# Transposing the gated product of nine FFN steps in 32x32 blocks on VectorE, with the blocks exchanged through memory

## What is computed

```
D_MODEL = 1024; SEQ = 256; DEPTH = 2; D_FF = 2816

def swiglu(x, w_in, w_out):
    gu = x @ w_in
    g, u = jnp.split(gu, 2, axis=-1)
    return (jax.nn.silu(g) * u) @ w_out
...
    for l in range(DEPTH):
        x = x + 0.5 * swiglu(rms_norm(x, ffn1_norm[l]), ffn1_w_in[l], ffn1_w_out[l])
        x = x + mixer(...)
        x = x + 0.5 * swiglu(rms_norm(x, ffn2_norm[l]), ffn2_w_in[l], ffn2_w_out[l])
...
        gate, up = jnp.split(h2 @ w_gate_up[l], 2, axis=-1)
        x = x + (jax.nn.silu(gate) * up) @ w_down[l]
```

## Time and profile before

| what | value |
|---|---|
| time, median of 3 runs | 1720.64 us (1720.05 to 1723.21) |
| span of the profiled execution | 1721.5 us |
| PE busy | 1671.8 us, 97% of the span |
| DVE busy | 943.5 us, 55% |
| ACT busy | 803.8 us, 47% |
| POOL busy | 97.1 us, 6% |
| DMA | 308.96 MB, 179 GB/s on average |

### The profile page before, as it was taken

How to read it: one execution, slowest core, us unless ns; L and a number is a source line. 1 busy time by engine, 2 the same in 40 slices (tenths; PEclk the granted TensorE clock), 3 DMA queues, 4 the chain that set the end, 5 groups by cost and what they waited for, 6 DMA issues and landing times.

```text
span 1721.5 us, 22066 instructions
## 1 busy us (share of the span) xinstructions
PE 1671.8 (97%) x7760; PEld 1376.7 (80%) x7760; DVE 943.5 (55%) x843; ACT 803.8 (47%) x899; POOL 97.1 (6%) x105
## 2 busy tenths in 40 slices
PE   6999999999999999999999999899999999999998
PEld 5887887888888787888888888787888878788886
DVE  4545545575545645465566545566554556665454
ACT  5443454544434543444455444465444446544443
POOL 2010000010000002000001000021100002110000
PEclk9999999999999999999999999999999999899999
DMA  8875453446565578555345655644456564336552
GB/s 259 295 221 175 172 190 123 139 156 199 176 208 188 175 251 240 174 173 181 111 152 166 203 188 194 240 127 129 141 190 200 179 195 144 125 127 201 189 192 89
DMA packets 209187, 308.96 MB, mean 179 GB/s; under 512 B 10400, under 2 KB 153504, under 8 KB 208480
## 3 DMA queue, kind: packets, MB, share of 16 engines
q1 hardware_dynamic: 208272, 305.18, 54.1%
q0 software_dynamic: 560, 1.84, 0.4%
q10 hardware_dynamic: 288, 1.05, 0.2%
HBM read 306.97 MB, written 2.88 MB: 180 GB/s over the span
## 4 chain that ended last, share of the span: by engine, by line
PE 90%; DVE 3%; ACT 3%; issue 2%; DMA 1%; POOL 1%; DVEq 0%; SPq 0%; ACTq 0%; POOLq 0%
PE pg L1380 19%; PE pg L1381 18%; PE pg L1382 18%; PE acc L1382 9%; PE acc L1380 9%; PE acc L1381 9%; PE pg L1451 2%; DVE wlo L970 2%; ACT whi L671 1%; DMA raw<-in_ffn_w_in 1%; PE pg L1393 1%; PE acc L1530 1%; PE acc L1550 1%; POOL ms L590 0%; PE acc L1538 0%
## 5 line engine op out<-in xcount | busy, mean ns | idle before, releaser
L970 DVE TENSOR_TENSOR wlo<-raw,whi 128x2048 fp32r<-128x2048 f32 x277 | 641.2, 2316 | 513.8 <-ACT whi L671 513.8
L671 ACT ACTIVATE whi<-raw 128x2048 fp32r<-128x2048 f32 x277 | 529.5, 1913 | 338.6 <-PE pg L1382 168.2
L1380 PE MATMUL pg<-whi,xTh 128*128 128x512 f32 (+1 forms) x1456 | 580.3, 399 | 9.9 <-DVE wlo L970 5.7
L1382 PE MATMUL pg<-whi,xTl 128*128 128x512 f32 (+1 forms) x1456 | 570.4, 392 | 0.0
L1381 PE MATMUL pg<-wlo,xTh 128*128 128x512 f32 (+1 forms) x1456 | 570.2, 392 | 0.0
L1380 PEld LDWEIGHTS pg<-whi,xTh 128*128 128x128 f32 x1456 | 276.3, 190 | 73.6 <-DVE wlo L970 9.8
L1382 PEld LDWEIGHTS pg<-whi,xTl 128*128 128x128 f32 x1456 | 276.0, 190 | 57.5
L1381 PEld LDWEIGHTS pg<-wlo,xTh 128*128 128x128 f32 x1456 | 276.5, 190 | 54.3
L1380 PE MATMUL acc<-whi,bTh 128*128 128x512 f32 (+1 forms) x572 | 229.6, 401 | 0.0
L1382 PE MATMUL acc<-whi,bTl 128*128 128x512 f32 (+1 forms) x572 | 224.3, 392 | 0.0
L1381 PE MATMUL acc<-wlo,bTh 128*128 128x512 f32 (+1 forms) x572 | 223.1, 390 | 0.0
(11 more groups left out here) (159 smaller groups left out, 1048.2 us busy)
## 6 DMA issues: line engine op xcount, KB each, us to landing
raw<-in_ffn_w_in SPq DMA_DIRECT2D x176, 512.0 KB, 4.8
raw<-in_ffn_w_out SPq DMA_DIRECT2D x88, 512.0 KB, 4.0
raw<-in_w_gate_up SPq DMA_DIRECT2D x88, 512.0 KB, 4.7
raw<-in_mix_w_in SPq DMA_DIRECT2D x64, 512.0 KB, 4.1
raw<-in_w_down SPq DMA_DIRECT2D x44, 512.0 KB, 4.0
raw<-in_w_in SPq DMA_DIRECT2D x24, 512.0 KB, 4.8
raw<-in_mix_w_o SPq DMA_DIRECT2D x16, 512.0 KB, 4.7
raw<-in_w_o SPq DMA_DIRECT2D x16, 512.0 KB, 4.5
```

Of the source, the lines that this page charges most:

```text
L671: act_e.activation(whi[:, slot, :], raw[:, slot, :], ACT.Copy).then_inc(s.w_hi_ready, 1)
L970: v.tensor_tensor(wlo[:, slot, :], raw[:, slot, :], f32(whi[:, slot, :]), ALU.subtract).then_inc(s.w_lo_ready, 1)
L1380: pe.matmul(dst, xh, wh, start=first and i == 0, stop=False)
L1382: mm = pe.matmul(dst, xl, wh, start=False, stop=last and i == len(pairs) - 1)
```

## The change

In each FFN the transposes by PE stay for steps 0 and 10 only. For steps 1 to 9 (`TURNED` = 9) the transpose is done in three moves. DVE transposes `act` within blocks of 32x32 into `turned` (`v.transpose`, one instruction over 128x512 elements), after the product of tile 1 and ahead of the low part of slot 0. ACT's queue then stores `turned` (256 KB) to a buffer in memory, `act_blocks`, waits for the store, and issues four loads of 32 partitions x 4 pieces x 512 bytes (64 KB each) that bring the blocks to their places in `moved` (`move`, after the refill of slot 0). After the refill of slot 1, ACT waits for the four loads and writes the high part from `moved` (`moved_hi`), DVE the low part (`moved_lo`); both used to stand ahead of the refill of slot 1. The high and low parts lie in another order in `bTh` and `bTl` (tile and channel block exchanged), under the names `actTh` and `actTl`.

```diff
+        turned, moved = area(11264, TT * FB), area(11776, TT * FB)
+        act_blocks = act.rearrange("p t (c b j) -> p b (t c) j", c=2, b=QUADS)
+        turned_blocks = turned.rearrange("p (b n i) -> p b n i", b=QUADS, n=TT * 2)
+        moved_blocks = moved.rearrange("p (a e) -> p a e", a=QUADS)
+        moved_T = moved.rearrange("p (a n i) -> p n a i", a=QUADS, n=TT * 2)
...
+        stored = nc.dram_tensor("act_blocks", (QUADS, Q, QUADS, TT * FB // QUADS), F32, kind="Internal").ap()
...
+                def moved_hi(j, par):
+                    act_e.wait_ge(s.act_moved, 16 * QUADS * (TURNED * f + j))
+                    act_e.activation(actTh[:, par].rearrange("p n (a i) -> p n a i", a=QUADS), moved_T,
                                      ACT.Copy).then_inc(s.actT_hi, 1)
...
+                def move(j):
+
+                    act_e.wait_ge(s.act_turned, TURNED * f + j)
+                    act_e.dma_start(stored.rearrange("a j b e -> (a j) (b e)"), turned).then_inc(s.act_stored, 16)
+                    act_e.wait_ge(s.act_stored, 16 * (TURNED * f + j))
+                    act_e.wait_ge(s.actT_lo, STEPS * f + j)
+                    for b in range(QUADS):
+                        act_e.dma_start(moved_blocks[Q * b:Q * (b + 1)], stored[:, :, b, :].rearrange("a j e -> j a e"))\
+                            .then_inc(s.act_moved, 16)
...
+                def moved_lo(j, par):
+                    v.wait_ge(s.actT_hi, STEPS * f + j + 1)
+                    hi, lo = (b[:, par].rearrange("p n (a i) -> p n a i", a=QUADS) for b in (actTh, actTl))
+                    v.tensor_tensor(lo, moved_T, f32(hi), ALU.subtract).then_inc(s.actT_lo, 1)
+
+                def step(j, par, turn=True):
+                    product(0, 1 - par, j + 1)
+                    refill(2, rnd + j + 1)
+                    product(1, 1 - par, j + 1)
+                    if turn:
+
+                        v.wait_ge(s.act_ready, 2 * STEPS * f + 2 * j + 4)
+                        v.transpose(turned_blocks, act_blocks).then_inc(s.act_turned, 1)
+                    refill(0, rnd + j + 2)
...
-                        if t == 0:
-                            turn(j + 1, 1 - par)
+                        if t == 0 and last:
+                            turn(STEPS - 1, 0)
```

More of the change, by code:

```diff
@@ L62 @@
 B_IN = 1952
+Q = 32
+QUADS = P // Q
+TURNED = STEPS - 2
 FFN_ROUNDS = STEPS
@@ new lines, in ffn @@
+                product_hi(0, pg[0][0])
+                refill(1, rnd + 1)
+                step(0, 0)
+                move(1)
+                with act_e.Fori(0, (STEPS - 3) // 2) as jj:
+                    for par in (1, 0):
+                        j = 2 * jj + 2 - par
+                        refill(1, rnd + j + 1)
+                        moved_hi(j, par)
+                        step(j, par)
+                        move(j + 1)
+                refill(1, rnd + STEPS - 1)
+                moved_hi(STEPS - 2, 1)
```

70 lines of the change are left out of this document (37 added, 33 removed).

## The result

The changed kernel takes **1752.49 us** (median of 4 runs, 1749.72 to 1754.60) against 1721.24 for the kernel before on the same chip: ratio **1.0177**, 95% interval 1.0165 to 1.0189. It is 1.8% slower where 1.9% faster was forecast, and outside the range of 1682 to 1706. The profiled execution spans 1752.7 us.

The account below looks back on a forecast made before the run. The FFN steps were taken as bound by PE (TensorE) alone. 1720.6 - 27.0 (54 turns of transposes removed) - 6.0 (two stalls) = 1687.6, said as 1688 us, with a range of 1682 to 1706.

Parts of the forecast that it names:

- the exchange's cover: Time to spare before the down projection: L1 + L2 may be 11.0 us, 7 expected, so a cover of 4.
- PE's part: On TensorE in the FFN steps: 54 turns of four transposes go, 27.0 us saved, and nothing is added.
- A turn: Four transposes of the gated product on TensorE, ahead of the down projection's second half: 0.50 us each, bounds 0.36 to 0.60.
- the two stalls: TensorE's turn waited 3.13 and 2.27 us beside GpSimd's mask pass; removing it was to gain 6 us, between 0 and 7.
- L1: Landing time of the exchange's 256 KB store to memory, taken as 3.5 us.
- L2: Landing time of the last of the exchange's four 64 KB loads, taken as 3.5 us.
- the sum less 11: Lateness of the down projection: L1 + L2 beyond the 11.0 us available; each us over was priced at 54 us.
- the 10.0 us of the bias loads: Upper bound for a landing: the bias table's loads of 512 KB while weights arrive, read from the earlier trace.
- rival (b): Exchange late only beside other loads, first FFN of two layers: 12 steps by 1 to 2 us, about 1706 us; chance 0.08.
- The gain of 33 us: The whole forecast gain: 27.0 us from transposes removed from TensorE plus 6 us from the two stalls.

Follow-up runs that it names:

- the direct exchange: The changed kernel with blocks moved from SBUF to SBUF in 16 transfers of 16 KB, 8 issued by ACT and 8 by SyncE, none through memory: 1722.12 us.

## Why the prediction was wrong, point by point

The step that failed is the exchange's cover: "a cover of 4" by one deadline, with both landings at 3.5 us, and a price of 12 to 24 us where other loads run. The runs showed 0.4 us or less in steady steps, by a second deadline on DVE, and a loss of 45.4 us in the two FFNs with other loads.

- **PE's part was right.** A turn is worth 0.50 us: 146.88 for nine steps without, 151.38 with. The 6 us from the two stalls are also there without the exchange: 156.23 - 147.52 - 4.5 = 4.2 in the first FFN and 153.78 - 148.16 - 4.5 = 1.1 in the third, together 5.3. The difference of the two profiled spans is 1721.5 - 1691.1 = 30.4; with the 3.4 us at the outer loop's return it would have been 33.8, against 33.0 forecast. By the median of its runs that version gains 22 us and not 30, so PE's part is right in each step, and 8 us over the whole stay open.
- **DVE's and ACT's durations were right:** the transpose 0.71 (0.7 taken), high part 0.63, low part 0.68, store's issue 0.35. The four loads' issues take 1.76 and not 1.48.
- **The landing times failed as a term.** L1 was taken as 3.5 and is 5.5 in steady steps, L2 3.5 and is 3.0. Their sum of 8.5 is still below 11. But with the last of the loads it is 7.39 + 6.15 = 13.5 in the first step that is late, and 9.62 + 6.85 = 16.5 in the sixth of the version without the mask pass. The formula itself, the sum less 11, makes these 2.5 and 5.5 us late; 2.82 and 5.86 were measured, 0.3 to 0.4 more, which is about the 0.3 that the issues take more. I had the 10.0 us of the bias loads as the upper bound and set it aside for the 4.9 of a transfer with nothing like them beside it. The fit that the Trainium skill gives (DMA: Bandwidth & Descriptors, section Anatomy of one DMA) had made L1 an estimate of 2.6. The page gives that fit for transfers issued by GpSimd, and these are issued by ACT. The trace doesn't agree, with 5.5, and 3.6 beside half the weights.
- **A second deadline was left out.** The prediction followed what is queued behind ACT's waits against PE's wants for the weight slots, and the product's low part against its own loads, but not the two together on DVE. There the low part of slot 1 stands ahead of the low part of the product. Store's landing, four issues 1.76, the refill's two passes 1.92 and 2.29 and the low part 0.68 stand in one row, so L1 alone may be about 5.5 + 0.4 = 5.9 us, whatever L2 is. This deadline rules the steady steps; in the late ones, the mask pass aside, the loads end last. It left the steady steps with hardly any cover, and 0.8 to 1.9 us were lost in each of three undisturbed FFNs (147.72, 148.77 and 148.05 against 146.88).
- **The mechanism that came was rival (b), at two to four times its price.** Its place was right: the first FFN of both layers. It was priced at 12 to 24 us. The exchange costs 24.5 + 20.9 = 45.4 there. Fewer steps were late than the 12 it counted, six in all, and each by more. With the mask pass left out their waits are 2.5 to 5.9 us and not 1 to 2, and sum to 23.3, just under the rival's upper price. Two things come on top. After each wait PE's clock is at the lower level for a while, and the next step is 1.5 to 2.4 us longer, 11.2 in all, a cost that the prediction had itself read from the earlier trace rows and not added to the rival. And GpSimd's mask pass, whose stall was booked as a gain of 6, moved to another pass of DVE where it costs 11.7 for both layers: the late refill brought them together.
- **One more place of the same kind was not seen.** The last exchange of the fourth FFN meets the loads for the last stage: a wait of 5.12 us, also with no other loads in the first FFN (FFN 4 takes 152.4 there too).
- **3.2 us at the first outer loop's return** were in no term; nothing in the trace of before showed them.
- **The chances.** (b) was given 0.08 with nearly all of its weight on the faster side. The gain of 33 us is used up at 12 steps x 2.75 us, and with both landings at the 10.0 of the earlier trace rows a step would have been 9 us late. The place was named and the rows were there; what was missing is the upper bound of the price, and with it a part of (b) on the slower side.

## What to carry to other kernels

A transfer's landing time is to be taken from transfers that run beside the same traffic, and its upper bound belongs in the price of every rival that rests on it. Where a change puts a wait in an engine's queue, follow each thing behind it to where the next engine's order brings it together with the new chain, and not only to its own user. And a resource that is freed earlier is refilled earlier: ask what that transfer will meet. Where an exchange is late only beside certain loads, keep the old way there: the direct exchange in all six FFNs changed nothing (1722.12 us), in four of the six it brought 0.6 to 0.7%.

## What the runs showed of the hardware that was not expected

- The same instructions of VectorE in another loop layout cost 3.2 us at the return of the first stack's outer loop: 2.48 us of standing with nothing to wait for (1.0023, 1.0009 to 1.0037 for the whole). The return of the second stack's loop shows no such gap.
- A store of 256 KB issued while four weight loads of 512 KB are being issued lands after 5.5 us, after 3.6 with half of the bytes in these loads, and after 9.5 with the bias table's loads beside it.
- Eight issues of 16 KB transfers take 5.0 us of ACT's or SyncE's queue, 0.63 each, against 0.35 for one store and 0.44 for each of four loads.
- A VectorE pass with two inputs in SBUF that starts together with GpSimd's pass of 8.8 us takes 10.95 us in place of 2.29: it ends 2.14 us behind GpSimd's pass, as if it had waited for that and then run at its own speed. The second such meeting in the same trace ends 2.15 us behind.
